# Key pages turned in place by VectorE, past scores in 32x32 tiles of TensorE, in a two-path decoder step

## The reference, cut to what matters

```python
# _fox_attend, for a sample sequence: q (8 tokens), k and v = 16 cache pages + 8 new rows, 16 heads of 64
s = einsum('nqhd,nkhd->nhqk', q, k) * HEAD_DIM ** -0.5
s = s + fq - fk                      # forget gates, a running sum over the keys
p = softmax(where(kpos <= qpos, s, -inf))
o = einsum('nhqk,nkhd->nqhd', p, v)
# layer: x + (o * silu(z)) @ w_out
```

## Time and profile before

| what | value |
|---|---|
| time, median of 3 runs | 977.95 us (977.21 to 978.5) |
| span of the profiled execution | 973.7 us, 4.3 us below the median time |
| TensorE busy | 935.6 us (96%) |
| weight loads of TensorE | 798.8 us |
| VectorE, ScalarE, GpSimd busy | 489.1, 384.8, 168.3 us |
| one step of `heads` | 66.2 us, of which TensorE is busy 65.3 |
| moved by DMA | 206.40 MB |

### The profile page before, as it was taken

The page is one execution under the profiler, slowest core; times in us unless marked ns, Lnnn a source line. Parts: engine busy times, 40 slices in busy tenths (PEclk is TensorE's granted clock), DMA queues, the critical chain, the costliest instruction groups (busy, mean ns, idle before and its releaser), DMA issues.

```text
span 973.7 us, 23729 instructions
## 1 busy us (share of the span) xinstructions
PE 935.6 (96%) x8516; PEld 798.8 (82%) x8516; DVE 489.1 (50%) x1133; ACT 384.8 (40%) x728; POOL 168.3 (17%) x111
## 2 busy tenths in 40 slices
PE   3899999999999999999999999999999999999998
PEld 2899999999998997758768768678687687786898
DVE  5744645555256434453554544644535545545732
ACT  5233333332135443453543544535435445436210
POOL 2243444331130221101102002012020020100000
PEclk8799999999999999999999999999999999999999
DMA  6222222322542525879799799798897997986412
GB/s 211 68 85 86 66 87 84 86 86 89 152 150 81 177 87 178 295 253 368 249 334 335 241 361 317 245 372 297 280 356 251 352 336 241 370 317 227 166 44 98
DMA packets 133188, 206.40 MB, mean 212 GB/s; under 512 B 8831, under 2 KB 91312, under 8 KB 133026
## 3 DMA queue, kind: packets, MB, share of 16 engines
q1 hardware_dynamic: 123538, 199.40, 60.7%
q10 hardware_dynamic: 9088, 4.46, 1.7%
q0 software_dynamic: 528, 2.10, 0.8%
HBM read 195.29 MB, written 10.63 MB: 211 GB/s over the span
## 4 chain that ended last, share of the span: by engine, by line
PE 84%; DMA 5%; DVE 4%; ACT 4%; issue 2%; SPq 0%; ACTq 0%; DVEq 0%
PE psum L1224 41%; PE psum L1194 17%; PE psum L1249 9%; PE psum L1382 7%; PE psum L1497 4%; DMA page_ring<-in_cache_k 4%; ACT sample_scores L708 2%; PE psum L1447 2%; DMA w_raw<-in_a_w_out 1%; PE psum L1425 1%; PE psum L1297 1%; PE psum L1405 1%; PE psum L1427 1%; PE psum L1429 1%; DMA constants<-in_table 0%
## 5 line engine op out<-in xcount | busy, mean ns | idle before, releaser
L1224 PE MATMUL psum<-xn_high,w_high 128*128 128x256 f32 x992 | 233.9, 318 | 2.6 <-DVE xn_low L821 2.6
L1224 PE MATMUL psum<-xn_low,w_high 128*128 128x256 f32 x992 | 213.6, 297 | 0.0
L1224 PE MATMUL psum<-xn_high,w_low 128*128 128x256 f32 x992 | 213.5, 297 | 0.0
L1224 PEld LDWEIGHTS psum<-xn_high,w_high 128*128 128x128 f32 x992 | 162.9, 191 | 19.6 <-issue 16.6
L1224 PEld LDWEIGHTS psum<-xn_high,w_low 128*128 128x128 f32 x992 | 168.1, 190 | 0.0
L1224 PEld LDWEIGHTS psum<-xn_low,w_high 128*128 128x128 f32 x992 | 168.0, 190 | 0.0
L1194 PE MATMUL psum<-constants,page_ring 128*128 128x128 f32 x1024 | 136.4, 276 | 6.3 <-DMA page_ring<-in_cache_k 5.0
L1194 PEld LDWEIGHTS psum<-constants,page_ring 128*128 128x128 f32 x1024 | 114.1, 140 | 33.4 <-issue 31.9
L503 POOL TENSOR_TENSOR w_raw<-w_raw,gains 128x1024 f32<-128x1024 f32 x32 | 60.7, 1897 | 339.2 <-DMA w_raw<-in_b_w_in 218.3
L1002 DVE COPY k_turned_odd<-psum 128x512 f32<-128x512 f32 x64 | 44.1, 690 | 93.1 <-PE psum L1194 93.1
L835 DVE TENSOR_TENSOR w_low<-w_raw,w_high 128x1024 fp32r<-128x1024 f32 x32 | 49.6, 1551 | 78.7 <-ACT w_high L565 78.7
(11 more groups left out here) (236 smaller groups left out, 1418.7 us busy)
## 6 DMA issues: line engine op xcount, KB each, us to landing
page_ring<-in_cache_k SPq DMA_DIRECT2D x128, 512.0 KB, 5.6
page_ring<-in_cache_v SPq DMA_DIRECT2D x128, 512.0 KB, 4.7
w_raw<-in_a_w_in SPq DMA_DIRECT2D x32, 512.0 KB, 4.0
suffix<-suffix_scratch SPq DMA_DIRECT2D x32, 256.0 KB, 4.6
w_raw<-in_b_w_in SPq DMA_DIRECT2D x16, 512.0 KB, 5.6
w_raw<-in_kv_w SPq DMA_DIRECT2D x16, 512.0 KB, 6.3
w_raw<-in_a_w_out SPq DMA_DIRECT2D x4, 1024.0 KB, 5.0
f_broad<-f_scratch SPq DMA_DIRECT2D x8, 512.0 KB, 6.0
```

The costliest lines, as they stand in the source:

```text
L1224: mm = pe.matmul(PS[:, bank + h, 0:c.stop - c.start], w[:, k, :], x[:, k, c], start=(k == 0 and n == 0), stop=(k == KT - 1 and n == 2))
```

## The change

1. **Turning.** The 16x8 transposes per step on TensorE, their copies and the tiles `k_turned` go. VectorE turns each key page in the ring itself, in 32x32 blocks: one `transpose` of 128x1024 per page.
2. **Scores.** `unit_scores` goes. `past_scores(r, between)`, r = 0 and 1, takes 8 pages at once: 128 matmuls of a 32x32 tile with 256 columns, over four row groups g and four column groups j; row group g writes bank T0+g, so all of T0, T1, C0 and C1. `take_scores(r)` on VectorE adds the forget values, four instructions of 256 columns.
3. **Queries.** `QC` takes another layout, filled by ScalarE with 16 small copies per step (`spread`), at the end of the step before.
4. **Order.** `project(0)` and `project(1)` stand together at the start of a step, then the first scores; then 7 pieces of `project(2)`, the last piece, the second scores. No piece is left for the second half. ScalarE's `high_b(KT + 3 * i + 3, 0)` moves from before the key copy to behind three DMA issues. VectorE's `low_b(KT + 3 * i + 3, 0)`, which waits for it, stays ahead of `block_max(0)`.
5. **Ring.** 16 slots. The key page of slot k is replaced by value page k once its round is scored (`b_scored`), the value page by the next sequence's key page once it is used. SyncE loads the next gate weights ahead of the first of those key pages, after waiting for the third `low_b` of the step.
6. **Late split.** The gated product of each step is only stored (in `QF`); high and low parts of all 8 are made in step 7. The spread queries `QZ` of the end stage are made by GpSimd during step 7.

```diff
@@ SyncE @@
         def heads(i, last):
+            sp.wait_ge(b_c0f, 4 * i)
+            sp.wait_ge(b_c1f, 4 * i)
+            src = f_dram[bass.ds(2 * i, 2), 0:SEQ].unsqueeze(0).to_broadcast([P, 2, SEQ])
+            sp.dma_start(FB[:, :, :], src).then_inc(b_fb, 16)
             for n in range(STREAM):
+                if n == 0 and not last:
                     sp.wait_ge(b_split, KT + 3 * i + 1)
                     load_w(wkv, (i + 1 + KT) * P, 0)
+                if n == 1:
+                    sp.wait_ge(b_taken, 8 * i + 4)
+                    load_suffix(i, 1)
+                if n == 8 and not last:
                     sp.wait_ge(b_split, KT + 3 * i + 3)
                     load_w(wkv, (i + 1) * P, 1)
...
+                if n == 16 and not last:
+                    sp.wait_ge(b_split, KT + 3 * i + 5)
+                    load_w(wqz, (i + 1 + KT) * P, 1)
...
+                if n < NPG:
+                    sp.wait_ge(b_scored, 2 * i + n // ROUND + 1)
+                else:
+                    sp.wait_ge(b_used, NPG * i + n - NPG + 1)
...
+                    load_page(i + n // NPG, (n + NPG) % STREAM)
@@ GpSimd @@
             scale_b(1, 6 + 2 * i, G_B)
-            if not last:
-                scale_b(0, 6 + i, G_KV)
             pool.wait_ge(b_rr, i + 1)
             pool.tensor_tensor(KN_T[:, :], KN_T[:, :], RR[:, :], ALU.mult).then_inc(b_normed, 1)
             if not last:
+                scale_b(0, 6 + i, G_KV)
                 scale_b(1, 7 + 2 * i, G_KV)
@@ ScalarE @@
-            for k in range(NPG):
...
-            if not last:
-                high_b(KT + 3 * i + 3, 0)
+            pr, sa = both(D0)
+            act.wait_ge(b_proj, KT + 3 * i + 1)
+            act.wait_ge(b_gf, i)
+            act.wait_ge(b_ddve, i + 1)
+            act.activation(prompt2(SQ[:, 0:SEQ]), pr, ACT.Square)
+            act.activation(SQ[:, SEQ:TOK], sa, ACT.Square).then_inc(b_dact, 1)
+            high_b(KT + 3 * i + 2, 1)
+            act.wait_ge(b_ss, i + 1)
...
+            act.wait_ge(b_proj, KT + 3 * i + 2)
+            act.activation(prompt2(VT[:, 0:SEQ]), pr, ACT.Copy)
+            act.activation(VT[:, SEQ:TOK], sa, ACT.Copy).then_inc(b_dact, 1)
...
             act.dma_start(k_sample.rearrange("b q h d -> (b q) (h d)")[:, cols], KN[0:NS, QB, :]).then_inc(b_kso, 16)
+            if not last:
+                high_b(KT + 3 * i + 3, 0)
...
+            else:
+                act.wait_ge(b_scored, 2 * i + 2)
+                spread(i + 1)
@@ VectorE @@
+            def turn_page(k):
+                dve.wait_ge(b_page[k], (2 * i + 1) * 16)
+                dve.transpose(ring[:, k, :], ring[:, k, :]).then_inc(b_turned, 1)
+            def take_scores(r):
...
+                if r == 0:
+                    dve.wait_ge(b_normed, i + 1)
...
+            for k in range(4):
+                turn_page(k)
+            dve.wait_ge(b_proj, KT + 3 * i + 1)
...
+            dve.tensor_scalar(KN_T[:, SEQ:TOK], sa, gk, None, ALU.mult).then_inc(b_ddve, 1)
+            for k in range(4, 6):
+                turn_page(k)
+            low_b(KT + 3 * i + 2, 1)
+            for k in range(6, 8):
+                turn_page(k)
+            for k in range(8, 11):
+                turn_page(k)
+            take_scores(0)
+            for k in range(11, NPG):
+                turn_page(k)
+            take_scores(1)
@@ TensorE @@
+                for h in range(4):
+                    for a in range(2):
+                        for j in range(4):
+                            for g in range(4):
+                                c = ((4 * j + h) * 2 + a) * 32
+                                mm = pe.matmul(
+                                    PS[32 * j:32 * j + 32, T0 + g, 0:ROUND * 32].rearrange("p (n k) -> p n k", k=32),
+                                    QC[32 * g:32 * g + 32, j, 64 * h + 32 * a:64 * h + 32 * a + 32],
+                                    ring[32 * g:32 * g + 32, ROUND * r:ROUND * r + ROUND, c:c + 32],
+                                    start=(h == 0 and a == 0), stop=(h == 3 and a == 1), tile_position=(32 * g, 32 * j))
+                mm.then_inc(b_scored, 1)
+            project(0, range(KT))
+            project(1, range(KT))
...
+            past_scores(0, lambda: sum_squares(OS, slice(SEQ, TOK)))
+            sum_squares(OP, slice(0, SEQ)).then_inc(b_ss, 1)
+            project(2, range(KT - 1))
+            past_scores(1, lambda: project(2, [KT - 1]))
```

More of the change, by code:

```diff
@@ L51 @@
 NEG = -1e30
-RING = 8
+RING = 16
+ROUND = 8
 STREAM = 2 * NPG
@@ L59, with held @@
 C_ALL = 1153
+H_ALL = C_ALL - NB * NS
+def held(c):
+    return c if c < C_NM else c - NB * NS
 G_A, G_KV, G_B, G_CONV, G_K, G_Q = 0, 8, 16, 24, 48, 49
@@ L198, in build @@
     QF = place("queries", [P, KT, TOK], over=at["gated_high"])
+    QZ = place("q_spread", [P, NB, KT, 32], over=at["sample_scores"])
     FA = place("f_raw", [H, TOK], over=at["k_t"])
@@ L366, in _ @@
             load_w(wqz, n * P, n % 2)
+        sp.wait_ge(s_rows, 16 * 9)
+        sp.wait_ge(s_cs, H)
+        for n in range(2):
+            load_page(0, n)
         for t in range(NT):
@@ L370, in _ @@
             sp.dma_start(h_dram[t * P:t * P + rows(t), :], X[0:rows(t), t, :]).then_inc(s_hst, 16)
+        for n in range(2, 7):
+            load_page(0, n)
         sp.wait_ge(s_co, 1)
@@ L384, in _ @@
         sp.wait_ge(s_xl, 2 * NT)
-        for n in range(RING // 2):
+        for n in range(7, 9):
             load_page(0, n)
@@ L759, in heads @@
                 high_slab(0)
+            else:
+                act.wait_ge(b_scored, 2 * i + 2)
+                spread(i + 1)
             ch.end()
-            assert t0[0] == 24
+            assert t0[0] == 8
+            if last:
+                act.wait_ge(b_used, NPG * i + 10)
+                for k in range(KT - 1):
+                    act.activation(G2H[:, k, 0:SEQ], QF[:, k, 0:SEQ], ACT.Copy).then_inc(b_gh, 1)
             act.wait_ge(b_used, NPG * (i + 1))
@@ L1369, in project @@
                     mm.then_inc(b_proj, 1)
-            def unit_scores(u):
-                full, free, bank = ((b_c0, b_c0f, C0), (b_c1, b_c1f, C1))[u % 2]
-                if u == 0:
-                    pe.wait_ge(b_qc, i + 1)
-                    pe.wait_ge(q_out, KT)
-                pe.wait_ge(free, 8 * i + u // 2)
-                pe.wait_ge(b_t0f, 24 * i + 2 * u + 2)
-                pe.wait_ge(b_t1f, 24 * i + 2 * u + 2)
-                for pp in range(2):
-                    for j in range(4):
-                        mm = pe.matmul(PS[32 * j:32 * j + 32, bank, 0:256], QC[:, 2 * j + pp, :],
-                                       KTS[u % 2][:, 2 * j + pp, :],
-                                       start=(pp == 0), stop=(pp == 1), tile_position=(0, 32 * j))
-                mm.then_inc(full, 1)
@@ L1387, in heads @@
-            for k in range(NPG):
-                pe.wait_ge(b_page[k % RING], (4 * i + k // RING + 1) * 16)
-                page = ring[:, k % RING, :]
-                free0()
-                for p in range(4):
-                    mm = turn(PS[:, T0, p * P:(p + 1) * P], page[:, p * P:(p + 1) * P])
-                mm.then_inc(b_t0, 1)
-                free1()
-                for p in range(4):
-                    mm = turn(PS[:, T1, p * P:(p + 1) * P], page[:, (4 + p) * P:(5 + p) * P])
-                mm.then_inc(b_t1, 1)
-                if k == 9:
-                    pe.wait_ge(b_dact, 2 * i + 1)
-                    pe.wait_ge(b_gf, i)
-                    pe.wait_ge(b_sot, i)
-                    pe.matmul(PS[:, OS, 0:NS], CT[:, C_ONESB:C_ONESB + P], SQ[:, SEQ:TOK], start=True, stop=True)
-                    pe.matmul(PS[:, OP, :], CT[:, C_ONESB:C_ONESB + P], SQ[:, 0:SEQ], start=True, stop=True).then_inc(b_ss, 1)
-                if k < 6:
-                    project(0, ([0, 1], [2, 3], [4], [5], [6], [7])[k])
-                if 7 <= k < 15:
-                    project(1, [k - 7])
-                if k % 2 == 0 and k >= 2:
-                    unit_scores(k // 2 - 1)
@@ new lines, in past_scores @@
+            def past_scores(r, between):
+                if r == 0:
+                    pe.wait_ge(b_qc, 16 * (i + 1))
+                    pe.wait_ge(b_t0f, 8 * i)
+                    pe.wait_ge(b_t1f, 8 * i)
+                    pe.wait_ge(b_c0f, 4 * i)
+                    pe.wait_ge(b_c1f, 4 * i)
+                else:
+                    pe.wait_ge(b_taken, 8 * i + 4)
+                pe.wait_ge(b_turned, NPG * i + ROUND * (r + 1))
+                between()
+                for h in range(4):
+                    for a in range(2):
+                        for j in range(4):
+                            for g in range(4):
+                                c = ((4 * j + h) * 2 + a) * 32
[5 more added lines that the diff above has]
+                mm.then_inc(b_scored, 1)
```

356 lines of the change are left out of this document (164 added, 192 removed).

## The result

The changed kernel takes **1160.9 us** (median of 4 runs, 1156.8 to 1163.1) beside 977.6 us for the kernel before on the same chip: 1.187 times the time, 95% interval 1.184 to 1.191. Slower, as forecast; but by 183 us where I forecast 77, and outside the range of 1005 to 1120. The profiled execution is the one of 1156.8 us, its span 1155.0.

The account below looks back on a forecast made before the run. TensorE bounds the kernel, DMA close behind; per step 16.4 us of work goes, some 24 us of waits come. Steps +45, late split +5 and clock +27 make 77 us on 977.95: 1055 us, range 1005 to 1120.

Parts of the forecast that it names:

- What bounds the kernel, and that TensorE loses its filler: TensorE, idle 0.9 us of a 66.2 us step, with DMA close (0.90); the change removes projection pieces interleaved with page turns.
- Block transposes 1.14 us: VectorE's 128x1024 turn of each key page: 1.14 us, ends 0.73 and 2.2; rival that they cost more, 0.06.
- Waits 1 to 5: TensorE waits before `project(1)` 5.8 us, `project(2)` 2.7, its last piece 3.0, key turns 2.1, fourth turned-probability group about 7.
- Tiles, 15.6 ns, 4.0 us per round: TensorE's 32x32 score tiles: 15.6 ns per record, 8.0 us per step, equal to the removed `unit_scores`; ends 13.9 and 62.5 ns.
- a round of tiles above 6 us: Profile sign that the forecast is wrong, at TensorE's past scores, where 4.0 us per round was expected.
- tiles cost more: Rival at TensorE's score tiles: 25 ns per record gives 1093 us, 31 ns about 1120, 62.5 ns 1250; chance 0.11.
- The clock, +27: TensorE's granted clock falls to half rate in 15 long waits, 1.8 us each on the mean: +27 us; rival without fall 0.14.
- waits 1 and 5: TensorE before `project(1)`, for late key pages, 6 us; before the fourth turned-probability group, behind `block_max(0)`, 7 us.
- wait 2: TensorE before `project(2)`, until ScalarE's copy of the values behind two logarithms and an exponential: 2.7 us.
- wait 3: TensorE before the last piece of `project(2)`, while VectorE takes four banks and turns five pages: 3.0 us.
- Late split +5: Step 7's 8 copies and 8 subtractions, mostly between the last product and the end stage: +5 us.
- TensorE sheds 16.4 us: Per step, 128 page-turning transposes at 0.128 us each leave TensorE: 16.4 us removed.
- The sum of 73.1: New step written out from the end of the last value product to the next: 73.1 us for 66.2, +6.9.

Follow-up runs that it names:

- the one-round kernel: Against the changed kernel, the two rounds of tiles made one, 128 products of 512 columns for 256 of 256, with the reordering this allowed: 1047.6 us.

## Why the prediction was right in sign and wrong in size

- *What bounds the kernel, and that TensorE loses its filler*: right. 96% became 80%.
- *Block transposes 1.14 us*: right; five in 5.74, 1.15 each; the end at 2.2 is out.
- *Waits 1 to 5, forecast 5.8, 2.7, 3.0, 2.1, 7*: 5.0, 2.3, 2.7, 1.8, 6.8. The held key pages and the moved `high_b` were shown by undoing each.
- *Tiles, 15.6 ns, 4.0 us per round, "adds nothing net in scores"*: **this is the step that failed.** The rounds took 8.9 and 8.2 us. The pace accounts for 1.7 of the 8.9 us lost per step and waits on issue for 5.2 (3.35 + 1.86). Of the remaining 2 us the clock explains about 0.7, in the second round, whose first 187 records came 22.8 ns apart at 0.69 to 1.00; the first ran at 1.00 (0.96 in its last stretch). The rest is the last record's own 0.4 us in front of each wait and behind each round. I counted 256 new records at their pace in the array and not as length of the program. Half of the tiles, and the same sums in half of the records, took the waits away; the kernel before with more records got them, at the heads of its steps. My test "a round of tiles above 6 us" named the failure; the rival "tiles cost more" had 0.11 and the wrong mechanism.
- *The clock, +27*: right that it falls. I counted falls at waits 1 and 5 alone; it also stood at 0.50 behind the first wait on issue and wait 2 (756 to 762) and at the last piece behind wait 3. In the timeline the stretches at half clock are 5.9 us per step longer than written, for the 3.4 allowed (27 / 8). What the clock costs by itself isn't shown to be that much: in the one-round kernel, full clock at two waits gave back 1.2 us a step.
- *GpSimd's scaling, moved behind the keys*: I didn't price it. It made a copy of 0.19 us last 1.76 us on the path, 13.6 us in all.
- *Late split +5*: right in size. The end stage waits 5.8 us for the queries, where it waited 0.42.
- *TensorE sheds 16.4 us*: misread. I took the last transpose's end for the next start; that is 0.2 us earlier:

```profile
640.23 0.51 PE L1224 MATMUL psum<-xn_high,w_high 128*128 128x256 f32 x2
```

From start to start the 16 pages took 13.4 us per step. The sum of 73.1 doesn't use the term, but its check does: 13.4 + 6.9 = 20.3 agrees with the five waits, which add to 20.6, where I wrote some 24. The waits that would leave the step as it was are 13.4 us, not 16.4. Two marks are also a few tenths off: 24.0 + 1.7 + 0.7 is 26.4, not 26.7, and 35.1 less 32.3 is 2.8, not 3.0.

The step that I followed is 17.4 us longer than written. Over 8 steps, less the 27 for the clock, that is 112, and 1055 + 112 = 1167 beside 1161 measured. The five waits that I had written out add nothing to the error, they are 18.6 us in all for 20.6; the instructions' arrival, the half clock and GpSimd do.

The Trainium skill ("Runtime: NRT & Kernel Launch", Instruction fetch mechanics) says that TensorE's instruction memory holds 2048 instructions, is filled in blocks of 16 KiB, and that a taken branch to code outside the current window stalls. The traces agree with the block (1.39 MB in 85 packets, 16.4 KB each) and with the stall. They don't agree with the page's window of two blocks: in the kernel before a whole step stays, without one packet. A record has a weight load beside it, so by an estimate 719 records are 1438 instructions, which stayed, and 847 are 1694, which didn't; the step's other instructions, which no row counts, come on top. The nine packets of a step are more than the eight blocks that 2048 instructions fill, which fits that limit; no run places it closer. The page also calls the cost of crossing blocks mostly hidden; here it wasn't, with 5.2 us in two rounds of short instructions. Nor do the runs show that going back to the start is all of it: the breaks inside the rounds come in step 0 too, where nothing is read again (0.25 and 2.15 us).

Open: why a record of 8 columns took 196 ns, and why the clock fell under them without idle time (with 64 of them in a step it was 153 ns, at a mean clock of 0.72); and what the second rounds and the heads of the steps would wait if no page loads ran beside them.

## What to carry to other kernels

When a change puts more, smaller instructions into a loop, count the loop's length as well as their time: read the instruction queue's bytes and the waits with no releaser, look at what else the DMA engines carry at that moment, and look for the form with the same sums in fewer records (512 columns for 256, with the reordering that it allowed, gave 113 us). When an engine's work is taken off a critical engine, what was interleaved with it becomes the path; move each queued item behind the work that doesn't need it before judging the idea. Savings of single edits don't add: read the next wait after each.

## What the runs showed of the hardware

- TensorE's program of a step stays in place with 719 records and is read again each time with 847. The price was 2.3 to 6.0 us at the head, and up to 4.4 us inside a run of 32x32 tiles.
- The wait for instructions in a first round of 256 columns was 0 to 0.8 us with the DMA engines idle (share 0.02) and 1.9 to 3.4 us with page loads on them (0.97 to 1.07).
- Tiles of 32x32 came 12.8, 19.0 and 32 ns apart with 128, 256 and 512 columns.
- A VectorE copy of 128x64 fp32 took 0.19 us alone and 1.76 beside a GpSimd product of 1.90 us.
- 128x128 products of 8 columns into one place of a bank came 196 ns apart, with the granted clock at 0.50 under most of them; a projection's records of 256 and 320 columns come 0.133 apart (48 in 6.40 us).
